# Index scores two heads side by side, fewer threshold rounds inside top-k, and softmax rows scaled on VectorE

## What is computed

```python
s = jnp.einsum('bthd,bsd->bths', qi, kidx)                   # index scores, 8 heads of 64
score = jnp.einsum('bths,bth->bts', jax.nn.relu(s), wi)
score = jnp.where(vis[None], score, -jnp.inf)
_, idx = lax.top_k(score, topk)                              # prompt: 132 of up to 528; sample: 256 of 2052
...
logits = jnp.einsum('btkgd,btjkd->btkgj', qg, k_sel) * (A_HEAD_DIM ** -0.5)
logits = jnp.where(valid[:, :, None, None, :], logits, -jnp.inf)
p = jax.nn.softmax(logits, axis=-1)
o = jnp.einsum('btkgj,btjkd->btkgd', p, v_sel)
```

## Time and profile before

| | |
|---|---|
| median of 3 runs | 1712.52 us (1712.36 to 1713.32) |
| the profiled execution | 1712.0 us, its span 1710.2 us |
| PE busy | 1589.6 us, 93% of the span, 11984 matmul records |
| DVE, ACT, POOL busy | 544.1, 554.1, 549.9 us, 32% each |
| chain that ended last | PE 84%, DVE 8%, ACT 4%, issue 2% |

### The profile page before, as it was taken

The page is one execution under the profiler, slowest core; times in us unless marked ns, Lnnn a source line. Parts: engine busy times, 40 slices in busy tenths (PEclk is TensorE's granted clock), DMA queues, the critical chain, the costliest instruction groups (busy, mean ns, idle before and its releaser), DMA issues.

```text
span 1710.2 us, 28405 instructions
## 1 busy us (share of the span) xinstructions
PE 1589.6 (93%) x11984; PEld 1484.9 (87%) x11984; DVE 544.1 (32%) x1089; ACT 554.1 (32%) x745; POOL 549.9 (32%) x206
## 2 busy tenths in 40 slices
PE   6896998898999999999889889999989999999996
PEld 6864866578999999999888887789989999999996
DVE  5269855632210101012316772233430111001113
ACT  4243245542432322223344332102333432222231
POOL 5410212513433343333354431002334333434240
PEclk9858998889999999999889987658989999999998
DMA  5322231132222223212221200034212222232221
GB/s 151 130 90 83 71 126 51 48 127 74 72 76 92 74 80 99 94 60 77 82 75 58 67 26 1 1 124 159 75 50 87 85 67 91 87 99 74 71 77 53
DMA packets 116840, 136.04 MB, mean 80 GB/s; under 512 B 5848, under 2 KB 111594, under 8 KB 114705
## 3 DMA queue, kind: packets, MB, share of 16 engines
q1 hardware_dynamic: 112949, 113.91, 21.2%
q0 software_dynamic: 3456, 20.97, 3.5%
q10 hardware_dynamic: 356, 0.03, 0.0%
HBM read 127.14 MB, written 7.94 MB: 79 GB/s over the span
## 4 chain that ended last, share of the span: by engine, by line
PE 84%; DVE 8%; ACT 4%; issue 2%; POOL 0%; ACTq 0%; DMA 0%; DVEq 0%; POOLq 0%
PE PS L1820 66%; PE PS L1917 2%; PE PS L2338 2%; PE PS L2375 2%; PE PS L2336 2%; DVE SC L1330 1%; DVE M L1324 1%; PE PS L2086 1%; PE PS L2370 1%; PE PS L2354 1%; PE PS L2304 1%; PE PS L1848 1%; PE PS L2010 1%; PE PS L2317 1%; DVE BC L1629 1%
## 5 line engine op out<-in xcount | busy, mean ns | idle before, releaser
L1820 PE MATMUL PS<-HHI,WHI 128*128 128x280 f32 x2304 | 647.8, 298 | 19.0 <-DVE HLO L1252 10.8
L1820 PE MATMUL PS<-HLO,WHI 128*128 128x280 f32 x2304 | 641.9, 295 | 0.0
L613 POOL TENSOR_TENSOR WLO<-RAW,WHI 128x2048 fp32r<-128x2048 f32 (+2 forms) x89 | 365.5, 4107 | 780.2 <-ACT WHI L825 590.4
L1820 PE MATMUL PS<-HHI,WLO 128*128 128x280 f32 x2304 | 489.9, 295 | 0.0
L1820 PEld LDWEIGHTS PS<-HHI,WHI 128*128 128x128 f32 x2304 | 444.2, 193 | 24.7 <-issue 14.8
L1820 PEld LDWEIGHTS PS<-HLO,WHI 128*128 128x128 f32 x2304 | 443.6, 193 | 0.0
L1820 PEld LDWEIGHTS PS<-HHI,WLO 128*128 128x128 f32 x2304 | 373.3, 192 | 0.0
L825 ACT ACTIVATE WHI<-RAW 128x2048 fp32r<-128x2048 f32 x87 | 166.1, 1909 | 149.0 <-PE PS L1820 146.0
L1820 PE MATMUL PS<-ALO,WHI 128*128 128x280 f32 x704 | 192.8, 291 | 0.0
L1820 PE MATMUL PS<-AHI,WHI 128*128 128x280 f32 x704 | 192.8, 291 | 0.0
L1595 DVE TENSOR_TENSOR AT<-PS,SG 128x560 f32<-128x560 f32 x44 | 32.6, 742 | 473.7 <-PE PS L1820 473.7
(11 more groups left out here) (327 smaller groups left out, 1674.1 us busy)
## 6 DMA issues: line engine op xcount, KB each, us to landing
RAW<-in_ffn_w_gate SPq DMA_DIRECT2D x22, 1024.0 KB, 5.2
RAW<-in_ffn_w_up SPq DMA_DIRECT2D x22, 1024.0 KB, 5.3
RAW<-in_ffn_w_down SPq DMA_DIRECT2D x16, 768.0 KB, 4.7
RAW<-in_w_in_odd SPq DMA_DIRECT2D x12, 1024.0 KB, 5.3
RAW<-in_ffn_w_down SPq DMA_DIRECT2D x16, 640.0 KB, 4.2
RAW<-in_w_in_even SPq DMA_DIRECT2D x7, 1024.0 KB, 5.3
RAW<-in_w_out_even SPq DMA_DIRECT2D x4, 1024.0 KB, 5.2
SIN<-in_state_gla SPq DMA_DIRECT2D x8, 512.0 KB, 3.9
```

The lines of the kernel that those rows point to most:

```text
L613: pool.tensor_tensor(WLO[:, par, 0:kc, :], RAW[:, par, 0:kc, :], WHI[:, par, 0:kc, :].bitcast(F32), ALU.subtract).then_inc(lo_done, 1)
L1820: ins = pe.matmul(acc[a][:, half, 0:HALF], w[:, slot, k, c0:c0 + P], x[:, k0 + k, HALF * half:HALF * half + HALF], start=first and n == 0 ...
```

## The change

- **Index scores:** the two heads of a pair are issued by halves in turn (head 0 first half, head 1 first half, then the second halves). They have four pairs of PSUM banks in place of two (`score_bank`), and PE waits for the Relu of the pair before the last.
- **Threshold rounds:** 14 of them stand inside top-k, two in each of its last seven rounds. PE has the totals of rounds 0 to 12 after steps 7, 11, 16, 20, 25 and so on to 61 of the slabs (`SEEK_STEPS`); the totals 13 to 32 stand in the key phase (`K_TOTALS`), two of them in steps 0, 4, 8 and 12, one in the others.
- **Attention:** `scale_rows` multiplies the two rows of exponentials in place, by two `tensor_scalar`, and `flip` is a plain transpose with the identity. `INV` is gone.
- **Order:** the last four steps of the sample mask move from units 0 to 3 to units 6 to 9. `sample_left` and the total of round 33 come one unit's row maxima, or logits, later. ACT takes one exponential of a column ahead of the key phase. POOL issues all four late value gathers before it splits the output projection's first slab. A few semaphores are merged.

```diff
-SEEK_EARLY, SEEK_FROM = 21, 10
+SEEK_EARLY, SEEK_FROM = 14, 10
...
+SEEK_STEPS = [7 + 9 * r // 2 for r in range(13)]
+K_TOTALS = [[r for r in range(len(SEEK_STEPS), 33) if (r - len(SEEK_STEPS)) * 4 // 5 == y] for y in range(16)]
...
+        def score_bank(n):
+
+            return (4 if n // 2 % 2 == 0 else 0) + 2 * (n % 2)
...
-            cached("v", 4)
+            for b in range(4, 8):
+                cached("v", b)
             lo_at(out0, 0, 0)
-            for b in range(5, 8):
-                cached("v", b)
...
+            act.activation(STS[:, 0, 0:1], IDN[:, 0:1], ACT.Exp)
             for y in range(16):
...
                     if r >= SEEK_FROM and i == 3:
-                        seek_round(3 * (r - SEEK_FROM))
+                        seek_round(2 * (r - SEEK_FROM))
                 for i in range(1, NRB):
                     take8(i, 8 * r + i)
-                    if r >= SEEK_FROM and i % 2 == 0:
-                        seek_round(3 * (r - SEEK_FROM) + i // 2)
+                    if r >= SEEK_FROM and i == 3:
+                        seek_round(2 * (r - SEEK_FROM) + 1)
...
-                if n >= 2:
-                    dve.wait_ge(pt_tr, n - 1)
-                dve.tensor_tensor(INV[0:m, n % 2, :, 0:m], IDN[0:m, 0:m].unsqueeze(1).to_broadcast([m, 2, m]),
-                                  ST[0:m, 1, 2 * n:2 * n + 2].unsqueeze(2).to_broadcast([m, 2, m]), ALU.mult).then_inc(p_ready, 1)
+                for x in range(2):
+                    v = PR[0:m, n % 2, x, 0:nk]
+                    ins = dve.tensor_scalar(v, v, ST[0:m, 1, 2 * n + x:2 * n + x + 1], None, ALU.mult)
+                ins.then_inc(p_ready, 1)
...
-            dve.wait_ge(nm_ready, NRB - 1)
             row_max(0)
+            row_max(1)
             sample_left()
-            row_max(1)
             scale_rows(0)
...
-                if n < 4:
-                    sample_mask(2 + n)
+                if 6 <= n < 10:
+                    sample_mask(n - 4)
...
-                for h in range(IH):
-                    n = IH * (i - 1) + h
-                    if n >= 2:
-                        pe.wait_ge(relu_done, n - 1)
-                    lo = 64 * (h % 2)
+                for c in range(IH // 2):
+                    n = IH * (i - 1) + 2 * c
+                    if n >= 4:
+                        pe.wait_ge(relu_done, n - 2)
                     for half in range(2):
-                        ins = pe.matmul(PS[0:m, 4 + 2 * (n % 2) + half, 0:nk // 2], QIT[lo:lo + 64, h // 2, RB * i:RB * i + m],
-                                        KID[lo:lo + 64, half * (nk // 2):(half + 1) * (nk // 2)], start=True, stop=True)
-                    ins.then_inc(il_ready, 1)
+                        for x in range(2):
+                            ins = pe.matmul(PS[0:m, score_bank(n + x) + half, 0:nk // 2], QIT[64 * x:64 * x + 64, c, RB * i:RB * i + m],
+                                            KID[64 * x:64 * x + 64, half * (nk // 2):(half + 1) * (nk // 2)], start=True, stop=True)
+                            if half:
+                                ins.then_inc(il_ready, 1)
...
-                        if step % 3 == 2 and step // 3 < SEEK_EARLY:
-                            row_total(step // 3)
+                        if step in SEEK_STEPS:
+                            row_total(SEEK_STEPS.index(step))
...
-                if 1 <= y <= 32 - SEEK_EARLY + 1:
-                    row_total(SEEK_EARLY + y - 1)
+                for r in K_TOTALS[y]:
+                    row_total(r)
...
-                        ins = pe.matmul(PS[0:kb, j // per, c:c + m], PR[0:m, n % 2, x, RB * j:RB * j + kb], INV[0:m, n % 2, x, 0:m], start=True, stop=True)
+                        ins = pe.transpose(PS[0:kb, j // per, c:c + m], PR[0:m, n % 2, x, RB * j:RB * j + kb], ident(m))
...
             logits(0)
-            row_total(33)
             pe.wait_ge(tks, CUT_STEPS)
             logits(1)
+            row_total(33)
             pe.wait_ge(tks, LEFT_STEPS)
```

More of the change, by code:

```diff
@@ L95 @@
 SCOLS = 4 * QCOLS
-CUT_STEPS = 5 + 2 * 31 + 3
+SEEK_STEPS = [7 + 9 * r // 2 for r in range(13)]
+K_TOTALS = [[r for r in range(len(SEEK_STEPS), 33) if (r - len(SEEK_STEPS)) * 4 // 5 == y] for y in range(16)]
+assert sum(K_TOTALS, []) == list(range(len(SEEK_STEPS), 33))
+CUT_STEPS = 7 + 2 * 31 + 3
 LEFT_STEPS = CUT_STEPS + 1
@@ L256, in trunk @@
         UO, _, uo_end = region("UO", [NS, 2, 512], F32, sc_at)
-        INV, _, inv_end = region("INV", [RB, 2, 2, RB], F32, uo_end)
-        assert inv_end <= pts_end
+        assert uo_end <= pts_end
         NM, _, _ = region("NM", [RB, NRB, LP], BF16)
@@ L368, in trunk @@
             sem(n) for n in ("kit_tr", "kit_ready", "ss_done", "sr_done", "comb_done", "comb_evac"))
-        tk, nm_ready, nm_final, tks, nms_ready, newscore = (sem(n) for n in ("tk", "nm_ready", "nm_final", "tks", "nms_ready", "newscore"))
+        tk, nm_ready, nm_final, tks, nms_ready = (sem(n) for n in ("tk", "nm_ready", "nm_final", "tks", "nms_ready"))
         part_count, row_count = (sem(n) for n in ("part_count", "row_count"))
         kvr_tr, kvr_ready, ue_tr, sp_ready, uo_ready = (sem(n) for n in ("kvr_tr", "kvr_ready", "ue_tr", "sp_ready", "uo_ready"))
-        u_zero, pool_step, pd_ready, y_done, yhi, ylo = (sem(n) for n in ("u_zero", "pool_step", "pd_ready", "y_done", "yhi", "ylo"))
+        pool_step, pd_ready, y_done, yhi, ylo = (sem(n) for n in ("pool_step", "pd_ready", "y_done", "yhi", "ylo"))
         lg_ready, mx_ready, exp_done, tail_done, p_ready, pt_tr, pt_evac, pv_done, ohi, olo = (
@@ L692, in _ @@
             pool.wait_ge(qis_ready, 4)
-            pool.memset(UE[:, :, 0:PB], 0.0).then_inc(u_zero, 1)
+            pool.memset(UE[:, :, 0:PB], 0.0).then_inc(pads_set, 1)
             step.mark(pool.memset(NM[:, 0, 0:RB], 0.0))
@@ L897, in _ @@
                         act.wait_ge(sc_done, n - 1)
-                    act.activation(RL[0:m, n % 2, 0:nk].rearrange("p (a n) -> p a n", a=2), PS[0:m, 4 + 2 * (n % 2):6 + 2 * (n % 2), 0:nk // 2], ACT.Relu).then_inc(relu_done, 1)
+                    act.activation(RL[0:m, n % 2, 0:nk].rearrange("p (a n) -> p a n", a=2), PS[0:m, score_bank(n):score_bank(n) + 2, 0:nk // 2], ACT.Relu).then_inc(relu_done, 1)
                     if n == 4:
@@ L953, in _ @@
                     if g == 0:
-                        act.wait_ge(u_zero, 1)
+                        act.wait_ge(pads_set, 4)
                     evac(s, j, UE[:, g, PB:PB + HALF], acc[j][:, 0, 0:HALF], False)
@@ L1352, in seek_count @@
                     dve.wait_ge(casts, 13)
[L1353 to L1356, removed]
+                    seeking(dve.tensor_tensor(new, new, VNF[3 * NS:P, 0:NS], ALU.mult))
+                    seeking(dve.tensor_tensor(new, new, VNF[3 * NS:P, NS:2 * NS], ALU.add))
                     dve.wait_ge(pads_set, 3)
@@ L1362, in total @@
             def total(r):
-                return PS[:, 7 if r < 33 else 1, 0:1]
+                return PS[:, 1 if r == 33 else 7, 0:1]
             def seek_update(r):
@@ L1410, in seek_round @@
                 seek_count(r)
+            assert 2 * (ROUNDS_P - SEEK_FROM) == SEEK_EARLY
             for r in range(1, ROUNDS_P):
@@ L1426, in _ @@
                 dve.tensor_scalar(NM[0:m, i, 0:nk], SC[0:m, i - 1, 0:nk], TAKEN_CUT, NEG, ALU.is_gt, ALU.mult).then_inc(nm_ready, 1)
-            assert 3 * (ROUNDS_P - SEEK_FROM) == SEEK_EARLY
             def sample_left():
@@ L1903, in _ @@
             pe.matmul(PS[:, 5, 0:NS], CA[0:8, C_A8:C_A8 + P], WIT[0:8, LP:R], start=True, stop=True).then_inc(wi_tr, 1)
-            pe.wait_ge(acc_free[1], 2)
+            pe.wait_ge(acc_free[1], 3)
             pe.wait_ge(wi_ready, 3)
@@ L1965, in row_total @@
                 pe.wait_ge(part_count, r + 1)
-                pe.matmul(PS[:, 7 if r < 33 else 1, 0:1], (PRIOR if r == 33 else SAME)[:, :, :].rearrange("p q n -> p (q n)"), SEEK[:, 2:3], start=True, stop=True).then_inc(row_count, 1)
+                pe.matmul(PS[:, 1 if r == 33 else 7, 0:1], (PRIOR if r == 33 else SAME)[:, :, :].rearrange("p q n -> p (q n)"), SEEK[:, 2:3], start=True, stop=True).then_inc(row_count, 1)
             def kv_rows(i):
```

## The result

The changed kernel takes 1708.2 us in the median of 20 executions where the kernel before takes 1712.4. Executions of either scatter over 16 to 22 us, so the medians, 4.1 us apart, are a rough measure; the ratio over all executions is 0.9945 with a 95% interval of 0.9922 to 0.9968, about 9 us faster. The prediction was 18 us faster, 1694, and 1684 to 1704: the sign is right, about half of the gain is missing. By the ratio the time is 1703, just inside the range; the median lies 4 us outside it. The profiled execution took 1708.0 us, its span 1706.2.

The account below looks back on a forecast made before the run. PE is busy in almost every stage, so only stretches where it waits or runs at half clock can shrink. 11 + 10.6 - 8 + 4.6 = 18.2 us off 1712.0 gives 1693.8, with the median's half us 1694; range 1684 to 1704.

Parts of the forecast that it names:

- Index scores, 11 saved: Score stage: alternating heads with two pairs in flight makes DVE the pace; 28.9 us becomes 17.9, bounds 7 to 12.
- Slabs, 10.6 saved, 6 to 14: Slabs with threshold rounds: shorter first wait 2.8, half clock 2 and 3, split stalls 1.2, eight fewer totals 1.6.
- key phase, 8 lost, 6 to 10: Key phase: four steps with a second total cost 7.2 us, the early exponential table load 0.7.
- Steady units, first turns, the slab's split: Attention: steady units nearly 0 (1 us saved over all twenty), shorter first turns 1 saved, first slab's moved split 6.6 saved.
- masks 2: Attention: sample mask steps moved to units 6 to 9 lie on the loop there; 2 us lost.
- conflict with GpSimd 2: Attention: scalings against GpSimd's pooling operations; 2 us lost, bound 0 to 6 (eight units, two scalings, 0.4 us each).
- My own two signs of error: Attention: prediction wrong if DVE's scalings take over 1 us next to GpSimd, or the clock is under 0.8.
- Behind 351 us I move it as it is: Everything after 351 us of the execution: nothing changed, so its length was taken as unaltered.
- Scores at half clock: Rival: half clock through the index scores, DVE not the pace, 4 us less gain there; 1699 us, chance 0.12.
- Doubled totals: Rival: clock falls in the key phase's idle, some eight steps grow by about 1 us each; 1702 us, chance 0.08.
- PE bound attention: Rival: attention is PE bound, its savings come through with no port conflict, 8 us more; 1686 us, chance 0.13.
- Transposes letting the clock fall: Rival: transposes in place of matmuls lower the attention's clock, up to 26 us over twenty units; 1720 us, chance 0.04.

Follow-up runs that it names:

- both2: The same kernel as `a_both`, run a second time; ratio 0.9913 to the kernel before.
- a_both: Changed kernel with the old turns and the mask steps back in units 0 to 3; ratio 0.9894 to the kernel before.
- a_mask: Changed kernel with the four mask steps back in units 0 to 3, scalings kept; ratio 0.9923 to the kernel before.
- a_mask2: The same kernel as `a_mask`, run a second time; 1701.3 us in one execution.
- a_inv: Changed kernel with the old turns (diagonal's small product and matmuls), mask steps still in units 6 to 9; ratio 0.9939 to the kernel before.
- a_inv2: The same kernel as `a_inv`, run a second time; 1705.9 us in one execution.
- both_nopool: Changed kernel with old turns, old mask place and GpSimd's pooling operations left out (pooled output missing); 1699.0 us in one execution.
- a_nopool: Changed kernel with GpSimd's pooling operations left out (pooled output missing); ratio 0.9893 to the kernel before.

## Why the prediction was right or wrong

- **Index scores, 11 saved: right.** 11.7 measured. Row tiles two to four take 18.3 us, from 86.35 to the end of the last adds at 104.66; forecast 17.9; the stall in the first tile stayed. The clock was 0.74, and DVE was the pace: a pair of 448 keys, which I had priced at 0.96 us of PE, took 1.01 (timeline, PE, 92.43) at a clock of 1.00, where four of DVE's adds took 3.05 (92.54).
- **Slabs, 10.6 saved, 6 to 14, and key phase, 8 lost, 6 to 10: right together, each too small.** Cut at the first key logits they read 11.6 saved (9.2 to 12.4 in the other traces) and 8.4 lost, but that cut puts the key phase's first step into the slabs. Cut where ACT's last copies of the slabs end (225.61 us before, 198.34 after), the slabs save 14.9 us (12 to 15 over the traces), a little beyond the range, and the key phase loses 11.7, or 9.3 where the clock held (`both2`). That the two errors cancel is luck. In the slabs the first total's wait went to 0.55 us where I had kept 2.7; two splits still hold the integer column, and the slack covers them wholly, where I had kept 2.8.
- **In the key phase** four waits of 1.33 us, the extra totals and the table load's 0.64 (I had 0.7) were the sum. The last total's wait for DVE, 1.09 us, was not in it. Nor were 3 to 6 us at a clock of 0.50 at the phase's start, which eight of the thirteen traces of changed kernels show; in the changed kernel the clock fell at about 201 us, after PE had been busy 2.5 of the 4 us from 196 to 200.
- **Steady units, first turns, the slab's split: right in sum.** 1.5 us saved in units 0 to 5 and 5.2 in units 13 and 14, where I had 2 and 6.6 (3 of it for a clock that falls a little later all the same). Of the 1.5 us 1.3 are in the first two units; a steady pooled unit of 448 keys lost 0.26. What stood at one place of the loop was wrong all the same: I closed the loop over the turn, where PE's gain cancels the scalings. The loop that binds runs over DVE and ACT alone; PE's gain is not in it, and the second scaling is.
- **The step that failed: masks 2 and conflict with GpSimd 2.** Units 6 to 10 lost 10.9 us where I had put these two terms at 4 together, and at 8 with the conflict at its bound. These 6.9 us too much are most of the 8.9 by which the attention missed (4.3 lost, not 4.6 saved), and the 8.9 are the missing half of the gain. The place was named (the scalings beside GpSimd's pooling, bound 0 to 6), but three things were missing in its size. A held pair takes 2.2 us more, not 0.4 per scaling, though only two pairs were held where I counted eight units. The mask steps are held as well, and they push other work to the start of a pooling operation; I had priced them by their own length. And what is held stands ahead of values on PE, with the clock at 0.74 behind it. The kernel before had the mask steps in units 0 to 3; in units 0 to 5 POOL is busy 1.9 us of 28, and that I didn't read. "Port conflict", as one rival calls it, is only a name: no run shows a port, they show operations that last longer beside GpSimd's, as 3.03 us for a pair in place of 0.82.
- **My own two signs of error both came:** scalings of 1.5 us each next to GpSimd, and a clock of 0.77 in the attention.
- **"Behind 351 us I move it as it is": 7.4 us off in the profiled execution.** 5.2 of them are in the chunk loop, at a clock of 0.65 in place of 0.70. Two executions of one program (`a_both`, `both2`) differ by as much there; whether the change has a part in it is open.
- **Rivals.** Scores at half clock: no. Doubled totals: 1.33 us each, and the clock did fall beside the first of them, for some 2.4 us in all (11.7 less 9.3), not the rival's 8. PE bound attention: no. Transposes letting the clock fall: not settled. Units 6 to 10 without pooling operations ran at 0.92 with transposes and at 1.00 with the old turns; with them, at much the same length, at 0.81 and 0.85 (`a_mask`, `a_mask2`) against 0.93 and 0.95 (`a_inv`, `a_inv2`). But PE also idles more in the first of each pair, and a clock as low as 0.61 was in six units of old turns too (`both_nopool`). No run here parts the transposes from the idle time.

By these runs the change is some 12 us of scores, 12 of slabs less 8 in the key phase (by the first cut), 3.5 in the attention for the moved split (89.6 to 86.1), and a scaling that gains nothing by itself and, with the moved masks, gives back some 8 us in the attention (93.92 and 94.86 against 86.1).

## What to carry to other kernels

Before work is put on VectorE, list the stretches in which GpSimd runs two-input operations on long rows (here adds of 128x692 in 1.34 to 1.5 us and splits of 128x2048 in some 4.5), and place it in the others: a pair of scalings took 3.03 us beside the adds and 0.82 without them. Cost a held instruction by the length of GpSimd's operation (the integer column of 0.16 us took 4.53 beside a split of 4.54), and add what waits behind it on its engine (3.59 and 4.26 us of PE here). Close the loop over the engines that are really in it before setting a gain on one engine against a cost on another. When two edits meet at one place, measure that place, not the whole stage.

## What the runs showed of the hardware

The DVE operations that were held in these traces ended with a GpSimd operation. In the kernel before, the integer column (176.64, 4.53 us) ended with a split (176.62, 4.54 us); in the changed kernel it ended at 162.34 and 179.04, the splits at 162.34 and 179.02. Two scalings of 0.41 us took 3.03 together, some 1.5 each, beside operations of 1.34 to 1.5 us (the pair ended at 286.92, GpSimd's second add at about 286.7). It showed on the other side too: GpSimd's small difference of 0.26 us took 0.83 while a DVE operation of 0.78 us with two SBUF inputs ran (300.01 to 300.79). Row maxima, which read PSUM, took 0.49 us beside GpSimd (304.05) and 0.50 without its operations (`a_nopool`, 287.54). One overlap looks otherwise: at 289.52 a pair of 336 keys took only 0.78 us (0.70 in `a_nopool`, 286.74) beside GpSimd's scaling of one input, which took 2.77 us in place of 1.92. So an in-place scaling can be held, which the prediction's bound of 0 to 6 us had left open. By what the two engines hold each other, no run shows.

In `both_nopool` PE's granted clock was 0.50 from 252 to 280 us with PE busy throughout (28.0 of 28 us), 0.87 from 280 to 284, and 1.00 from 284; in the eight us ahead of that stretch PE had been busy for 3.7. Units 0 to 5 ran at 0.68 on average over 34 us in `a_inv`, and at 0.86 in the same instructions of `a_inv2`. Why one execution leaves 0.50 earlier than another, no run here settles.
